# Differential attention: four of eight heads turned by VectorE's blocks and a trip through memory in place of TensorE's transposes

## The reference, cut to what matters

```python
q = rope(rms_norm(q.reshape(..., nh, 2, dh), g_q))    # k the same way
s = jnp.einsum('bhtqd,bhtkd->bhtqk', q_blk, kt) * scale
pr = jax.nn.softmax(s, axis=-1)
a = pr[:, :, 0] - lam * pr[:, :, 1]                   # 256 x 256 for each head
o = jnp.einsum('bhqk,bhkd->bhqd', a, vt)
o = rms_norm(o, g_sub) * (1.0 - lambda_init)
return o.reshape(bsz, seq, D_MODEL) @ w_out
```

## Time and profile before

| | |
|---|---|
| time, median of 3 runs | 888.64 us (888.57 to 890.1) |
| the profiled execution | 889.01 us, its span 887.2 us |
| TensorE busy | 882.0 us (99%) |
| VectorE busy | 673.0 us (76%) |
| ScalarE busy | 502.6 us (57%) |
| GpSimd busy | 80.3 us (9%) |
| granted TensorE clock | full in all slices |

### The profile page before, as it was taken

One profiled execution on the slowest core, in us unless ns is written; L12 is line 12 of the kernel. 1 busy time (PEld: TensorE's weight loads), 2 busy tenths in 40 slices (PEclk: granted clock), 3 DMA queues, 4 the chain that ended last, 5 costly groups with the idle time before them and its releaser, 6 DMA issues.

```text
span 887.2 us, 12026 instructions
## 1 busy us (share of the span) xinstructions
PE 882.0 (99%) x4286; PEld 729.0 (82%) x4286; DVE 673.0 (76%) x1041; ACT 502.6 (57%) x820; POOL 80.3 (9%) x92
## 2 busy tenths in 40 slices
PE   9999999999999999999999999999999999999998
PEld 8988888888888888778888888888888888887777
DVE  6997688666746699997787666645879987779863
ACT  6666464444535576787564444444665445577681
POOL 1002010000000403111100000000010000115300
PEclk9999999999999999999999999999999999999999
DMA  9754568676667566423387666775777774757701
GB/s 341 264 179 177 202 259 304 237 272 243 244 217 241 213 233 242 144 98 117 128 301 261 244 241 239 253 242 179 255 294 256 240 243 158 292 169 244 234 23 48
DMA packets 85315, 194.51 MB, mean 219 GB/s; under 512 B 7300, under 2 KB 38404, under 8 KB 85256
## 3 DMA queue, kind: packets, MB, share of 16 engines
q1 hardware_dynamic: 83544, 189.15, 61.2%
q0 software_dynamic: 1280, 3.93, 1.4%
q10 hardware_dynamic: 432, 0.66, 0.2%
HBM read 175.23 MB, written 18.48 MB: 218 GB/s over the span
## 4 chain that ended last, share of the span: by engine, by line
PE 93%; DVE 5%; issue 1%; DMA 1%; ACT 0%; DVEq 0%; ACTq 0%
PE bank L1871 83%; PE bank L1909 3%; DVE wlo L1134 2%; PE bank L2186 1%; PE bank L2266 1%; PE bank L1924 1%; PE bank L2296 1%; DVE df_m L1552 1%; DVE df_tok L1556 1%; DVE df_stat L1576 1%; DMA h<-x_dram 1%; DVE df_ss L1528 1%; PE bank L2160 0%; PE bank L2252 0%; PE bank L2075 0%
## 5 line engine op out<-in xcount | busy, mean ns | idle before, releaser
L1134 DVE TENSOR_TENSOR wlo<-raw,whi 128x1024 fp32r<-128x1024 f32 x295 | 346.7, 1214 | 30.5 <-ACT whi L723 30.1
L723 ACT ACTIVATE whi<-raw 128x1024 fp32r<-128x1024 f32 x295 | 301.6, 1059 | 111.5 <-PE bank L1871 101.1
L1871 PE MATMUL bank<-whi,x_hi 128*128 128x512 f32 x560 | 152.4, 394 | 0.0
L1871 PE MATMUL bank<-wlo,x_hi 128*128 128x512 f32 x560 | 149.9, 389 | 0.0
L1871 PE MATMUL bank<-whi,x_lo 128*128 128x512 f32 x560 | 149.8, 389 | 0.0
L1871 PEld LDWEIGHTS bank<-wlo,x_hi 128*128 128x128 f32 x560 | 105.1, 188 | 22.2
L1871 PEld LDWEIGHTS bank<-whi,x_lo 128*128 128x128 f32 x560 | 105.1, 188 | 22.0
L1871 PEld LDWEIGHTS bank<-whi,x_hi 128*128 128x128 f32 x560 | 103.6, 188 | 22.7 <-issue 1.8
L1871 PE MATMUL bank<-whi,y_hi 128*128 128x512 f32 x396 | 107.6, 394 | 0.1
L1871 PE MATMUL bank<-whi,y_lo 128*128 128x512 f32 x396 | 106.1, 390 | 0.0
L1871 PE MATMUL bank<-wlo,y_hi 128*128 128x512 f32 x396 | 106.0, 389 | 0.0
(11 more groups left out here) (260 smaller groups left out, 891.9 us busy)
## 6 DMA issues: line engine op xcount, KB each, us to landing
raw<-stream_dram SPq DMA_DIRECT2D x295, 512.0 KB, 4.7
ffn_blocks<-ffn_blk SPq DMA_DIRECT2D x22, 256.0 KB, 2.2
ffn_land<-ffn_blocks SPq DMA_DIRECT2D x22, 256.0 KB, 4.2
residual_blocks<-h_blk SPq DMA_DIRECT2D x20, 256.0 KB, 2.0
h_land<-residual_blocks SPq DMA_DIRECT2D x20, 256.0 KB, 3.0
mb_blocks<-p_tok POOLq DMA_DIRECT2D x10, 192.0 KB, 3.8
mb_pT<-mb_blocks POOLq DMA_DIRECT2D x10, 192.0 KB, 4.3
cv_blocks<-cv_blk SPq DMA_DIRECT2D x7, 256.0 KB, 4.0
```

What stands on the lines that cost most here:

```text
L723: A(whi[:, u % RING, :], raw[:, u % SLOTS, :], ACT.Copy).then_inc(sem("w_hi"), 1)
L1134: V.tensor_tensor(wlo[:, u % SLOTS, :], raw[:, u % SLOTS, :], whi[:, u % RING, :].bitcast(F32), ALU.subtract).then_inc(sem("w_lo"), 1)
L1871: last = T.matmul(bank[pair + t][:, :], lhs[a][:, kt, t * P:(t + 1) * P], w[:, place(w, u), kk * NW:(kk + 1) * NW], start=part != 1 and k ...
```

## The change: what it does

- Heads 0, 2, 3 and 4 are no longer turned by TensorE. After `soft` a new step `blk` on VectorE transposes `a` in blocks of 32x32 (two instructions of 128x256), GpSimd issues the block's way to memory (`out`) and back into a landing tile (`in`), and ScalarE copies the landed tile to `df_aT`, in its old step `aT`. Heads 1, 5, 6 and 7 go as before. Waits that meant "head turned" now mean "blocks made" for the four. The landing tile lies under the part of X that is not yet written, the block tile under the per-layer inputs.
- `rope` turns both token halves in one step, side by side: all four swaps, then both products, then both sums. `more` is gone.
- `df_max` takes both halves of a head with one reduction over two banks, 128x1024, and one small product. The exponentials wait for both.
- The orders are written anew: `sums` 1 stands ahead of `rope` 1, `rope` 3 ahead of `soft` 1; TensorE's `qkT` 5 stands in unit 18 and `aT` 1 in unit 19; ScalarE's copies stand further back. The copy of head 3 stands between exponentials 6 and 7, that of head 4 behind `df_out` of heads 2 and 3.

```diff
+DF_TRIPS = (0, 2, 3, 4)
+DF_TURNED = tuple(_h for _h in range(8) if _h not in DF_TRIPS)
...
     "pe": (
-        (13, "scores", 0), (13, "scores", 1), (16, "scores", 2), (16, "aT", 0), (18, "qkT", 4), (18, "scores", 3), (18, "aT", 1),
-        (19, "qkT", 5), (20, "qkT", 6), (20, "qkT", 7), (20, "scores", 4), (20, "aT", 2), (21, "scores", 5),
-        (21, "av", 0), (21, "aT", 3), (21, "av", 1), (21, "scores", 6), (22, "scores", 7), (22, "aT", 4),
+        (13, "scores", 0), (13, "scores", 1), (16, "scores", 2), (18, "qkT", 4), (18, "qkT", 5), (18, "scores", 3),
+        (19, "aT", 1), (20, "qkT", 6), (20, "qkT", 7), (20, "scores", 4), (21, "scores", 5),
+        (21, "av", 0), (21, "av", 1), (21, "scores", 6), (22, "scores", 7),
...
     "act": (
-        (13, "qkT", 3), (14, "scores", 0), (15, "scores", 1), (16, "tile", 3), (16, "aT", 0), (16, "scores", 2),
-        (18, "qkT", 4), (18, "aT", 1), (18, "scores", 3), (18, "qkT", 5), (19, "qkT", 6), (19, "qkT", 7),
-        (20, "tile", 4), (20, "scores", 4), (20, "aT", 2), (20, "scores", 5), (20, "aT", 3), (21, "av", 1),
-        (21, "scores", 6), (21, "aT", 4), (24, "scores", 7), (24, "pair", 0), (24, "tile", 5), (24, "av", 3),
-        (24, "aT", 5), (25, "aT", 6), (26, "av", 5), (26, "aT", 7), (26, "pair", 1), (27, "av", 7), (28, "pair", 2),
+        (13, "qkT", 3), (14, "scores", 0), (15, "scores", 1), (16, "tile", 3), (16, "scores", 2),
+        (18, "qkT", 4), (18, "qkT", 5), (18, "aT", 0), (18, "aT", 1), (18, "scores", 3), (19, "qkT", 6), (19, "qkT", 7),
+        (20, "tile", 4), (20, "scores", 4), (20, "scores", 5), (21, "av", 1),
+        (21, "aT", 2), (21, "scores", 6), (22, "aT", 3), (24, "scores", 7), (24, "pair", 0), (24, "tile", 5), (24, "av", 3),
+        (24, "aT", 4), (24, "aT", 5), (25, "aT", 6), (26, "av", 5), (26, "aT", 7), (26, "pair", 1), (27, "av", 7), (28, "pair", 2),
...
     "dve": (
-        (5, "rope", 0), (6, "more", 0), (6, "sums", 0), (8, "rope", 1), (8, "sums", 1), (8, "more", 1),
-        (9, "unit", 1), (11, "sums", 2), (11, "rope", 2), (11, "more", 2), (11, "scores", 0), (12, "scores", 1),
-        (13, "soft", 0), (16, "unit", 2), (17, "scores", 2), (17, "soft", 1), (17, "rope", 3), (17, "scores", 3),
-        (17, "sums", 3), (17, "more", 3), (18, "soft", 2), (19, "scores", 4), (19, "soft", 3), (19, "scores", 5),
-        (19, "soft", 4), (21, "scores", 6), (22, "osums", 0), (22, "scores", 7), (22, "norm", 0), (22, "soft", 5),
+        (5, "rope", 0), (6, "sums", 0), (8, "sums", 1), (8, "rope", 1),
+        (9, "unit", 1), (11, "sums", 2), (11, "rope", 2), (11, "scores", 0), (12, "scores", 1),
+        (13, "soft", 0), (13, "blk", 0), (16, "unit", 2), (17, "scores", 2), (17, "rope", 3), (17, "soft", 1), (17, "scores", 3),
+        (17, "sums", 3), (18, "soft", 2), (18, "blk", 2), (19, "scores", 4), (19, "soft", 3), (19, "blk", 3), (19, "scores", 5),
+        (19, "soft", 4), (19, "blk", 4), (21, "scores", 6), (22, "osums", 0), (22, "scores", 7), (22, "norm", 0), (22, "soft", 5),
...
     "pool": (
-        (4, "sums", 0), (8, "sums", 1), (12, "sums", 2), (16, "sums", 3), (21, "osums", 0), (24, "osums", 1),
+        (4, "sums", 0), (8, "sums", 1), (12, "sums", 2), (13, "out", 0), (14, "in", 0), (16, "sums", 3), (18, "out", 2), (19, "out", 3), (19, "in", 2),
+        (20, "in", 3), (20, "out", 4), (21, "osums", 0), (21, "in", 4), (24, "osums", 1),
...
+            def df_out(hd):
+                n = DF_TRIPS.index(hd)
+                pool.wait_ge(sem("mb_blk"), n + 1)
+                nc.gpsimd.dma_start(a_dram[n], ablk[:, n % 2, :]).then_inc(sem(f"mb_out{n % 2}"), 16)
+            def df_in(hd):
+                n = DF_TRIPS.index(hd)
+                pool.wait_ge(sem(f"mb_out{n % 2}"), 16 * (n // 2 + 1))
+                if n >= 2:
+                    pool.wait_ge(sem("df_aT"), DF_COPIED.index(DF_TRIPS[n - 2]) + 1)
+                nc.gpsimd.dma_start(aland[:, n % 2, :].rearrange("p (i w) -> p i w", i=P // B),
+                                    a_dram[n].rearrange("q n -> (q n)").rearrange("(i p w) -> p i w", i=P // B, p=P))\
+                    .then_inc(sem(f"mb_land{n % 2}"), 16)
...
             def df_copy(hd):
-                act.wait_ge(sem("df_aT_filled"), hd + 1)
+                if hd in DF_TRIPS:
+                    n = DF_TRIPS.index(hd)
+                    act.wait_ge(sem(f"mb_land{n % 2}"), 16 * (n // 2 + 1))
+                    A(daT[:, hd % 4, :].rearrange("p (n i b) -> p n i b", n=4, b=B),
+                      aland[:, n % 2, :].rearrange("p (i n b) -> p n i b", n=4, b=B), ACT.Copy).then_inc(sem("df_aT"), 1)
+                    return
...
             def df_max(hd):
-                for m in range(2):
-                    dve.wait_ge(sem("df_scores"), 2 * hd + m + 1)
-                    V.tensor_reduce(stt[:, 2 * m:2 * m + 2], bank[DF_S_BANKS[hd][m]][:, :].rearrange("p (q k) -> p q k", q=TT),
-                                    AXX, ALU.max).then_inc(sem("df_max"), 1)
+                dve.wait_ge(sem("df_scores"), 2 * (hd + 1))
+                V.tensor_reduce(stt[:, 0:4].rearrange("p (m q) -> p m q", m=2),
+                                psum[:, b:b + 2, :].rearrange("p m (q k) -> p m q k", q=TT), AXX, ALU.max)\
+                    .then_inc(sem("df_max"), 1)
...
+            def df_blocks(hd):
+                n = DF_TRIPS.index(hd)
+                dve.wait_ge(sem("df_a"), TT * (hd + 1))
+                if n >= 2:
+                    dve.wait_ge(sem(f"mb_out{n % 2}"), 16 * (n // 2))
+                for q in range(TT):
+                    last = V.transpose(ablk[:, n % 2, :].rearrange("p (f k q b) -> p q f k b", f=P // B, q=TT, b=B)[:, q],
+                                       DF_P[hd][:, 0, q, :].rearrange("p (k b f) -> p f k b", b=B, f=P // B))
+                last.then_inc(sem("mb_blk"), 1)
```

More of the change, by code:

```diff
@@ L171 @@
     "pool": (
-        (4, "sums", 0), (8, "sums", 1), (12, "sums", 2), (16, "sums", 3), (21, "osums", 0), (24, "osums", 1),
+        (4, "sums", 0), (8, "sums", 1), (12, "sums", 2), (13, "out", 0), (14, "in", 0), (16, "sums", 3), (18, "out", 2), (19, "out", 3), (19, "in", 2),
+        (20, "in", 3), (20, "out", 4), (21, "osums", 0), (21, "in", 4), (24, "osums", 1),
         (26, "osums", 2), (28, "osums", 3),),
 }
+DF_COPIED = tuple(arg for _, step, arg in DF_ORDER["act"] if step == "aT")
 DF_SCORED_AT = {arg: u for u, step, arg in DF_ORDER["pe"] if step == "scores"}
@@ L267, in sem @@
             return sems[name]
-        bank = [ctx.enter_context(nc.psum_tensor(f"bank{b}", [P, NW], F32)) for b in range(8)]
+        psum = ctx.enter_context(nc.psum_tensor("bank", [P, 8, NW], F32))
+        bank = [psum[:, b, :] for b in range(8)]
         whi = sb("whi", [P, RING, 2 * NW], F32R)
@@ L277, in build @@
         h = sb("h", [P, TT, D])
+        landing = ExitStack()
+        sb("under_df_land", [P, 3 * D], scope=landing)
+        aland = sb("df_land", [P, 2, NW], scope=landing)
+        landing.close()
         X = (sb("x_hi", [P, KT, SEQ], F32R), sb("x_lo", [P, KT, SEQ], F32R))
         Y = (sb("y_hi", [P, KT, SEQ], F32R), sb("y_lo", [P, KT, SEQ], F32R))
+        staging = ExitStack()
+        ablk = sb("df_blk", [P, 2, NW], scope=staging)
+        staging.close()
         PT = (sb("p_hi", [P, 2, SEQ], F32R), sb("p_lo", [P, 2, SEQ], F32R))
@@ L651, in df_onorm @@
                     .then_inc(sem("df_orstd"), 1)
-            for _, what, arg in df_order("pool"):
-                if what == "sums":
+            def df_out(hd):
[10 more added lines that the diff above has]
+                    .then_inc(sem(f"mb_land{n % 2}"), 16)
+            for _, what, arg in df_order("pool"):
+                if what == "out":
+                    df_out(arg)
+                elif what == "in":
+                    df_in(arg)
+                elif what == "sums":
                     for k in range(TT):
@@ L1536, in head_unit, with df_rope @@
                                     ALU.mult).then_inc(sem(signal), 1)
[L1538 removed]
+            def df_rope(t):
                 w = (0, 1, 1, 0)[t]
[L1541 to L1543 removed]
+                for k in range(TT):
+                    x5 = dtok[:, t % 2, k, :].rearrange("p (a m u e) -> p a m u e", a=4, m=2, u=2)
                     m5 = dm2[:, k, :].rearrange("p (a m u e) -> p a m u e", a=4, m=2, u=2)
                     sn = rot[:, w, 1, k, :].rearrange("p (m u e) -> p m u e", m=2, u=2)
[L1546 to L1547 removed]
                     dve.wait_ge(sem("df_in"), TT * t + k + 1)
@@ L1554, in df_rope @@
                             .then_inc(sem("df_swap"), 1)
+                for k in range(TT):
+                    x3 = dtok[:, t % 2, k, :].rearrange("p (a e) -> p a e", a=4)
                     dve.wait_ge(sem("df_swap"), 2 * (TT * t + k + 1))
-                    V.tensor_tensor(x3, x3, cs, ALU.mult).then_inc(sem("df_cos"), 1)
+                    V.tensor_tensor(x3, x3, rot[:, w, 0, k, :].unsqueeze(1).to_broadcast([P, 4, P]), ALU.mult)\
```

(11 more changed lines are left out.)

45 lines of the change are left out of this document (24 added, 21 removed).

## The result

The changed kernel took 891.19 us (median of 22 executions, 889.34 to 892.13) against 888.67 for the kernel before beside it. By these medians it is slower by 2.5 us (0.28%), where 1.2 were forecast; it lies inside the range of 887.0 to 891.6 and near its upper end. The times lie in two groups, which makes the medians jump: the means differ by 1.6 us, and the ratio of the two kernels' executions is 1.002, 95% interval 1.0014 to 1.0026. One execution of the kernel before, at 3157 us, is left out of the means and the ratio.

A forecast was written before the change was run, and what follows sets the result against it. TensorE bounds the kernel, but unit 24 meets VectorE's chain through ScalarE: maximum 6 +1.3, latency +0.53, exponential 6 +1.8, less 0.63 slack, gives 888.64 + 1.2 = 889.8 us; range 887.0 to 891.6, the forecast's own 889.3 to 890.3.

The forecast's parts named there:

- The place and the mechanism: Unit 24, first product of the output matrix, waits for VectorE's chain through exponentials 6, 7 and `x_hi`; 1.2 us later.
- ScalarE's steps between are the same: From exponential 6 to `x_hi`: exponential 7 and `x_hi` start as much later as exponential 6, 1.8 us (1.3 to 2.3).
- the 0.63: At unit 24: slack against ScalarE in the kernel before, from `x_hi`'s end at 406.50 to the start at 407.13.
- The terms of VectorE: Up to maximum 6: blocks +4.72, rotations −1.84, maxima −1.50, `sums` 1 +0.5, vanished idle −0.58; +1.3 us (0.8 to 1.8).
- TensorE by itself would be at most 2.2 us earlier: Ahead of unit 24: four `aT` steps leave TensorE, 1.68 us, and the 0.5 us wait for the last rotation goes.
- The 0.5 us for the rotation: TensorE's longest wait, before `qkT` 6, goes because rotation 3 now stands ahead of softmax 1; 0.5 us.
- it stands idle some 2.5 to 3 us: TensorE ahead of unit 24: idle 2.5 to 3 us; work behind it is the same and nothing gives time back.
- The chances: Whole kernel: forecast 0.50; faster by over 0.2% 0.12, slower 0.28, no difference 0.60.
- Rival 1: At unit 24: TensorE's saving is cashed, 888.64 − 2.2 = 886.4 us; chance 0.12.
- Rival 2: VectorE's chain no longer than today, with cheap rotation and maxima; unit 24 starts 0.6 us earlier, 888.0 us; chance 0.14.
- Rival 3: Head 3's trip through memory becomes the last wait if it lands after 402.7; 1.9 us late, 891.7 us; chance 0.14.
- Rival 4: VectorE's rotation: side by side brings nothing, four rotations stay at 4.26, 1.84 us more, 891.6 us; chance 0.10.

The follow-up runs named there:

- the kernel with ScalarE's order: Changed kernel with only ScalarE's order altered: of three `whi` between exponentials 6 and 7, one moved ahead of 6, one behind head 4's copy; 887.95 us, ratio 0.999.
- the kernel without trips: Kernel before with only the side-by-side rotation, joint maxima and order of `sums` 1; TensorE turns all heads; 888.55 us against 888.70, ratio 0.9996.
- the serial rotation: Changed kernel with the rotation's instructions one block after the other again; 891.88 us, ratio 1.0032.
- the run with two slots: Changed kernel with two slots for the sums of squares, odd tiles having their own place; 891.42 us, ratio 1.0034.
- maxima by halves: Changed kernel with a head's maximum taken in two instructions of 512 columns again, instead of one of 1024; 891.15 us, ratio 1.0029.
- filled: Changed kernel with seven unused 128x128x128 products into free bank 4 between `av` 3 and unit 24; 889.75 us, ratio 1.0011.
- both edits: Changed kernel with two slots for the sums and ScalarE's altered order together; 889.75 us, ratio 1.0012.

## Why the prediction was right, and what it missed

- **The place and the mechanism** were right. Exponential 6 starts at 399.46 (forecast 399.5, from 397.71), `x_hi` at 407.17 (407.5), unit 24 at 408.29, 1.16 us later (1.2). The ten executions of the lower group have a median of 889.8 us, the forecast itself.
- **That it fits so closely is luck.** The two traces differ by 0.31 us ahead of the stage; counted from there unit 24 is 1.47 us later, still inside the forecast's 0.7 to 1.7. "ScalarE's steps between are the same" was 0.24 us off: from exponential 6 to `x_hi` 7.71 us pass, where it was 7.95, as the three `whi` take less time. And not all of the 0.63 was slack: unit 24 starts 0.26 us after `x_hi` ends (0.25 to 0.26 in all seven kernels in which `x_hi` comes last). The last two cancel.
- **The terms of VectorE.** Rotation 3.75 us (3.80), a maximum 362.37 − 361.05 = 1.32 (1.33), blocks 1.07 and 0.12 behind the softmax (1.18), latency to exponential 6 1.52 (1.50). In `sums` 1 VectorE waited 0.93 us: the forecast took 0.5, the middle between two ends, and the far end (0.96) was right. The gains of 0.50 a rotation and 0.26 a maximum, each a little larger than forecast, give about half of these 0.4 us back. The outlier among the powers was no outlier, since the power of 2.67 us comes back in every trace (344.18 above).
- **TensorE's idle time.** 2.5 to 3 us were forecast ahead of unit 24; there were 1.95, and another 0.53 + 0.65 upstream. The step that fell short is that "TensorE by itself would be at most 2.2 us earlier": it starts `av` 2 only 1.04 us earlier (404.39 instead of 405.43). The 0.5 us for the rotation did go, but the order that took them away sets softmax 1 behind rotation 3 and `aT` 1 behind `qkT` 5, and a wait of 0.53 us came in their place; the wait ahead of scores 4 grew from 0.25 to 0.65. This cost nothing, as unit 24 waited anyway; but the kernel with ScalarE's order has the same two waits (0.60 and 0.66 us), and they are most of why it gained 0.7 us and not 2.2.
- **The missing term** is the clock. The step "it stands idle some 2.5 to 3 us. Behind unit 24 its work is the same and nothing gives the time back" took the work behind the idle time at its old price. In nine of 22 executions it cost about 1.6 us more, and that moved the median from 889.8 to 891.2. The chances left this term out: the outcome lies on the line of 0.2% that they drew (0.28% by the medians, 0.2% by the ratio), and not well inside it.
- **The rivals.** Rival 1 (saving cashed) fell: it needs `x_hi` sooner, which came 1.5 us later; with ScalarE's order 0.7 us are had, but the kernel without trips reaches unit 24 as early. Rival 2 fell with the terms. Rival 3 fell: writes landed after 2.4 to 5.3 us and reads after 3.6 to 4.5, and no copy waited for one. Rival 4 fell with the serial rotation.

## What to carry to other kernels

When work is taken off the engine that bounds a kernel, find the next instruction of that engine that needs another engine's result, and count that chain: here it was ready 0.63 us ahead, so without a shorter chain all but these 0.63 us of TensorE's saving could only become idle time. Then look at the order of the engine in between before anything else: taking two splits out of ScalarE's way from exponential 6 to `x_hi` was worth 1.8 us (889.8 to 887.95), more than the 1.68 us of transposes taken off TensorE. And idle time on TensorE can have a price of its own: work behind it may run at the lower clock. Here two idle microseconds were worth filling even with work that nobody needs, as long as they could not be removed.

## What the runs showed of the hardware

**GpSimd's power beside VectorE's rotation.** The same two powers of 128x8, beside rotation 2, took 3.41 us in the kernel before, 5.77 in the changed one, and 3.41 again with the rotation one block after the other (5.77 also without trips, where the rotation is side by side). Changed kernel first, with the last two instructions of VectorE's rotation, then the serial rotation:

```profile
356.85 5.77 POOL L657 TENSOR_TENSOR df_ss<-df_ss,neg_half 128x8 f32<-128x8 f32 x2 [6.55 <-DVE df_ss L1574]
359.84 1.28 DVE L1606 TENSOR_TENSOR df_tok<-df_tok,df_m 128x512 f32<-128x512 f32 x2
```

```profile
357.46 3.41 POOL L657 TENSOR_TENSOR df_ss<-df_ss,neg_half 128x8 f32<-128x8 f32 x2 [6.65 <-DVE df_ss L1574]
```

Side by side VectorE's instructions leave no gap between them, and GpSimd is held up; with a dependent successor each time there is a gap of about 0.04 us. Alone such a power takes 1.64 us, the longest one took 6.12 in the run with two slots. It gets on only when VectorE's run is over: the second power of the changed kernel, begun at 358.5 in the middle of the rotation, ends at 362.62, 1.50 us after the rotation (361.12); the first of the run with two slots ends at 352.95, 1.49 us after the `wlo` that closes VectorE's run there (351.46). The Trainium skill, "SBUF — State Buffer", section "Who interferes with whom", says that a VectorE instruction with two inputs in SBUF contends with a GpSimd instruction that reads SBUF. The traces agree, as the rotation's instructions and `wlo` are of that kind. That the gaps are what lets GpSimd in is my reading of these rows; no run tested it by itself. In the changed kernel nothing waits for the longer powers beside rotation 2; with two slots VectorE waits for those beside rotation 1. The prediction had taken the cheaper rotation as free of a price.

**The clock.** Idle times of 2.10 us (serial rotation) and 1.69 us (maxima by halves) ahead of unit 24 left the clock at 1.00 in the profiled executions; 1.95 us in the changed kernel's and 2.00 with two slots did not. In the changed kernel 13 of 22 executions kept it, with two slots three of five: such an idle time is a chance, not a certainty, of the lower level. With 1.69 us none of seven executions shows a lower mean clock, and in the four kernels with at most 0.37 us there (filled, both edits, ScalarE's order, no trips) none of 44. Three of the changed kernel's twelve long executions show a mean clock of 1.00, and seven of 24 of the kernel before, in the last round, lie between 889.6 and 890.5 at 1.00 as well; what lengthens these is open.
